# Two half borders in place of one: a chain of twelve layers on one core

## What is computed

```
for layer in range(2):                      # first_block
    h = rms_norm(x, norm_g[layer, 0]) * (1 + scale) + shift
    x = x + 0.5 * gate * swiglu(h, ffn_w_in[layer, 0], ffn_w_down[layer, 0])
    h = rms_norm(x, norm_g[layer, 1]) * (1 + scale) + shift
    y = diff_attention(h, ...) if layer == 0 else hgrn2(h, ...)
    x = x + gate * y
    h = rms_norm(x, norm_g[layer, 2]) * (1 + scale) + shift
    x = x + 0.5 * gate * swiglu(h, ffn_w_in[layer, 1], ffn_w_down[layer, 1])
h = rmsnorm(x, norm_g_2)                    # second_block
x = x + concat(gla, sparse attention, pool) @ w_out
return rmsnorm(x, final_norm_g)

rms_norm(h, g) = h * rsqrt(mean(h * h, axis=-1) + 1e-6) * g
swiglu(h, w_in, w_down): a, b = split(h @ w_in); (silu(a) * b) @ w_down     # d_ff = 2816
```

## Time and profile before

| | us |
|---|---|
| median of 3 runs | 2433.12 (2431.3 to 2435.06) |
| span of the profiled execution | 2435.2 |
| PE busy | 2385.0 (98%) |
| weight loads | 1908.2 (78%) |
| DVE busy | 1273.8 (52%) |
| ACT busy | 861.1 (35%) |
| POOL busy | 203.1 (8%) |

### The profile page before, as it was taken

How to read it: one execution, slowest core, us unless ns; L and a number is a source line. 1 busy time by engine, 2 the same in 40 slices (tenths; PEclk the granted TensorE clock), 3 DMA queues, 4 the chain that set the end, 5 groups by cost and what they waited for, 6 DMA issues and landing times.

```text
span 2435.2 us, 30379 instructions
## 1 busy us (share of the span) xinstructions
PE 2385.0 (98%) x11030; PEld 1908.2 (78%) x11030; DVE 1273.8 (52%) x1951; ACT 861.1 (35%) x1320; POOL 203.1 (8%) x337
## 2 busy tenths in 40 slices
PE   7999999999899999999999999999999999999998
PEld 4888888677588888888888878888888888867666
DVE  5886334455568883343333345554533333459554
ACT  3222223566443222232232243434432222344353
POOL 1212000000001110000000013331000000021100
PEclk9999999999999999999999999999999999999999
DMA  7899432321149983323333321222233333242221
GB/s 267 272 288 290 118 95 66 102 61 52 48 126 290 294 251 109 94 76 93 102 95 107 92 78 54 60 56 75 78 104 95 100 112 95 65 96 55 64 58 52
DMA packets 420386, 285.27 MB, mean 117 GB/s; under 512 B 22691, under 2 KB 397789, under 8 KB 420305
## 3 DMA queue, kind: packets, MB, share of 16 engines
q1 hardware_dynamic: 397888, 207.64, 29.4%
q0 software_dynamic: 20896, 73.80, 9.2%
q10 hardware_dynamic: 1520, 2.77, 0.3%
HBM read 281.85 MB, written 6.72 MB: 118 GB/s over the span
## 4 chain that ended last, share of the span: by engine, by line
PE 91%; DVE 3%; ACT 2%; DMA 1%; issue 1%; SPq 1%; POOL 0%; ACTq 0%; DVEq 0%; POOLq 0%
PE bank L666 13%; PE bank L667 13%; PE bank L668 13%; PE bank L834 7%; PE bank L836 7%; PE bank L835 7%; PE bank L1442 4%; PE bank L1444 4%; PE bank L1443 4%; PE bank L1469 2%; PE bank L701 2%; PE bank L703 2%; PE bank L702 1%; PE bank L1087 1%; PE bank L1114 1%; PE bank L681 1%
## 5 line engine op out<-in xcount | busy, mean ns | idle before, releaser
L624 DVE TENSOR_TENSOR w_lo<-raw,w_hi 128x1024 fp32r<-128x1024 f32 (+1 forms) x333 | 435.7, 1309 | 430.3 <-ACT w_hi L606 425.7
L606 ACT ACTIVATE w_hi<-raw 128x1024 fp32r<-128x1024 f32 (+1 forms) x333 | 371.8, 1117 | 479.9 <-PE bank L668 243.0
L666 PE MATMUL bank<-h_hi,w_hi 128*128 128x512 f32 x1344 | 523.1, 389 | 1.8 <-DVE w_lo L624 1.8
L667 PE MATMUL bank<-h_lo,w_hi 128*128 128x512 f32 x1344 | 522.9, 389 | 0.0
L668 PE MATMUL bank<-h_hi,w_lo 128*128 128x512 f32 x1344 | 522.8, 389 | 0.0
L666 PEld LDWEIGHTS bank<-h_hi,w_hi 128*128 128x128 f32 x1344 | 252.3, 188 | 55.3 <-DVE w_lo L624 2.7
L668 PEld LDWEIGHTS bank<-h_hi,w_lo 128*128 128x128 f32 x1344 | 252.3, 188 | 52.4
L667 PEld LDWEIGHTS bank<-h_lo,w_hi 128*128 128x128 f32 x1344 | 252.3, 188 | 52.0
L834 PE MATMUL bank<-g_hi,w_hi 128*128 128x512 f32 x704 | 277.8, 395 | 0.0
L836 PE MATMUL bank<-g_hi,w_lo 128*128 128x512 f32 x704 | 276.0, 392 | 0.0
L835 PE MATMUL bank<-g_lo,w_hi 128*128 128x512 f32 x704 | 273.2, 388 | 0.0
(11 more groups left out here) (407 smaller groups left out, 3056.5 us busy)
## 6 DMA issues: line engine op xcount, KB each, us to landing
raw<-in_ffn_w_in SPq DMA_DIRECT2D x176, 512.0 KB, 3.9
ada<-in_ada_w POOLq DMA_DIRECT2D x128, 512.0 KB, 5.0
raw<-in_ffn_w_down SPq DMA_DIRECT2D x64, 704.0 KB, 4.6
raw<-in_hgrn_w_in SPq DMA_DIRECT2D x32, 512.0 KB, 4.1
raw<-in_attn_w_qkv SPq DMA_DIRECT2D x24, 512.0 KB, 3.8
raw<-in_w_in SPq DMA_DIRECT2D x22, 512.0 KB, 3.8
ada_first<-in_ada_w SPq DMA_DIRECT2D x16, 512.0 KB, 10.8
bias_scratch<-bias_lines POOLq DMA_DIRECT2D x14, 320.0 KB, 9.1
```

The source lines that it names most:

```text
L606: line(nc.scalar.activation(w_hi[:, n % 2, 0:k * P], raw[:, n % 4, 0:k * P], ACT.Copy), hi_ready)
L624: line(nc.vector.tensor_tensor(w_lo[:, n % 2, 0:k * P], raw[:, n % 4, 0:k * P], w_hi[:, n % 2, 0:k * P].bitcast(F32), ALU.subtract), lo_ready)
L666: nc.tensor.matmul(out_ap, wh, xh, start=(k == 0), stop=False)
L667: nc.tensor.matmul(out_ap, wh, xl, start=False, stop=False)
```

## The change

Each border is now worked in two parts of 256 tokens. The last output block of an FFN (the last two of WO and HO) is multiplied first for tokens 0 to 255, into one bank, then for tokens 256 to 511, into another. Between the tiles of the second part TensorE runs the ones matmuls of the first (`sums_pe(pe, m, 0)`). ACT and DVE do residual, square, root, scaled tiles and high and low parts for the first part while TensorE multiplies the second. The next stage's first two blocks are multiplied for the first part (block N over 8 tiles, then N+1), with the ones matmuls of the second part before tile 4, and then for the second part, both blocks tile by tile as before (`pair_both`). The orders of ACT and DVE at a border are written out in `border_act` and `border_dve`, with the splits of N and N+1 among them. `idle_turns` is gone. The square of block j = 0 goes straight to `sumsq`, so its memset and one add go. The rolled loops of ACT and DVE over the down blocks are written out, and TensorE's covers j = 0 to 5. `POOLED` is empty, so the GpSimd code added does not run. Semaphore counts change to suit; those lines are left out below.

```diff
+        BORDER = {1: "F0", 2: "WO", 3: "F1", 4: "F2", 5: "HO", 6: "F3"}
+        STAGES = ("F0", "WO", "F1", "F2", "HO", "F3", "OUT")
+        TAKEN = {"WO": 10, "HO": 10}
+        ADDED = {"WO": 7, "HO": 7}
...
+        def half_bank(j, half):
+            if j == KD - 1:
+                return B[6] if half else B[3]
+            return B[4] if half else B[2]
+        def root_bank(half):
+            return B[7] if half else B[5]
...
+            if j == 0:
+                return
...
+            line(nc.scalar.activation(sq[:, :] if j else sumsq[:, :], xT[:, j, :], ACT.Square), sq_ready)
...
+        def residual_half_dve(dve, line, j, half):
+            c_ = cols_of(half)
+            line(nc.vector.scalar_tensor_tensor(out=xT[:, j, c_], in0=half_bank(j, half)[:, c_], scalar=gate_col[:, j:j + 1],
+                                                in1=xT[:, j, c_], op0=ALU.mult, op1=ALU.add), x_ready)
+        def add_half_dve(dve, line, half):
+            c_ = cols_of(half)
+            dve.wait_ge(sq_ready, line.value(x_ready))
+            line(nc.vector.tensor_tensor(sumsq[:, c_], sumsq[:, c_], sq[:, c_], ALU.add), sum_ready)
+        def square_half_act(act, line, count, j, half):
+            c_ = cols_of(half)
+            act.wait_ge(x_ready, count)
+            line(nc.scalar.activation(sq[:, c_], xT[:, j, c_], ACT.Square), sq_ready)
...
+        def pair_tile(pe, m, half, k, b, banks):
+            c_ = cols_of(half) if m else slice(0, T)
+            n = FIRST[NEXT[m]] + b
+            wh, wl = w_hi[:, n % 2, k * P:(k + 1) * P], w_lo[:, n % 2, k * P:(k + 1) * P]
+            pe.wait_ge(hhi_ready, tile_count(m, half, k))
+            nc.tensor.matmul(banks[b][:, c_], wh, h_hi[:, k, c_], start=(k == 0), stop=False)
+            nc.tensor.matmul(banks[b][:, c_], wl, h_hi[:, k, c_], start=False, stop=False)
+            pe.wait_ge(hpool_ready if pooled(m, k) else h_ready, low_count(m, half, k))
+            return nc.tensor.matmul(banks[b][:, c_], wh, h_lo[:, k, c_], start=False, stop=(k == KD - 1))
+        def pair_both(pe, m, half, banks):
+            for k in range(KD):
                 for b in range(2):
-                    s = (n + b) % 2
-                    nc.tensor.matmul(banks[b][:, :], w_hi[:, s, k * P:(k + 1) * P], xh, start=(k == 0), stop=False)
-                    nc.tensor.matmul(banks[b][:, :], w_lo[:, s, k * P:(k + 1) * P], xh, start=False, stop=False)
-                pe.wait_ge(h_ready, KD * m + k + 1)
-                for b in range(2):
-                    s = (n + b) % 2
-                    last = nc.tensor.matmul(banks[b][:, :], w_hi[:, s, k * P:(k + 1) * P], xl, start=False,
-                                            stop=(k == KD - 1))
+                    last = pair_tile(pe, m, half, k, b, banks)
...
+            xb = x_base(BORDER[m]) + TAKEN.get(BORDER[m], 9)
+            pe.wait_ge(lo_ready, n + 1)
+            pe.wait_ge(x_ready, xb - 1)
+            for k in range(KD):
+                if k == 4:
+                    sums_pe(pe, m, 1)
+                pair_tile(pe, m, 0, k, 0, banks)
+            pe.wait_ge(lo_ready, n + 2)
+            pe.wait_ge(x_ready, xb)
+            for k in range(KD):
+                pair_tile(pe, m, 0, k, 1, banks)
+            pair_both(pe, m, 1, banks)
...
-        def idle_turns(count):
-            for _ in range(count):
-                nc.tensor.matmul(B[7][:, 0:P], ones[:, :], ones[:, :], start=True, stop=True)
-        def norm_pe(pe, m):
-            pe.wait_ge(sum_ready, (KD - 1) * m)
-            nc.tensor.matmul(B[5][:, :], ones[:, :], sumsq[:, :], start=True, stop=False)
-            idle_turns(4)
...
+        def sums_pe(pe, m, half):
+            name, c_ = BORDER[m], cols_of(half)
+            sums = sum_base(name) + ADDED.get(name, 6)
+            squares = x_base(name) + TAKEN.get(name, 9)
+            pe.wait_ge(sum_ready, sums - 1 if halved(m) and half == 0 else sums)
+            nc.tensor.matmul(root_bank(half)[:, c_], ones[:, :], sumsq[:, c_], start=True, stop=False)
+            pe.wait_ge(sq_ready, squares if half else x_base(name) + KD)
+            nc.tensor.matmul(root_bank(half)[:, c_], ones[:, :], sq[:, c_], start=False, stop=True).then_inc(rms_ps, 1)
...
+        def border_act(act, line, m, after):
+            name = BORDER[m]
+            n, xb = FIRST[NEXT[m]], x_base(name)
+            split_hi(act, line, n - 1)
+            nc.scalar.preload_act_table_set("natural_log_exp_and_others")
+            if halved(m):
+                square_half_act(act, line, xb + 7, KD - 2, 0)
+                square_half_act(act, line, xb + 8, KD - 1, 0)
+                norm_root_act(act, line, m, 0)
+                norm_hi_act(act, line, m, 0, 0)
+                split_hi(act, line, n)
+                square_half_act(act, line, xb + 9, KD - 2, 1)
+                norm_hi_act(act, line, m, 0, 1)
+                norm_hi_act(act, line, m, 0, 2)
+                split_hi(act, line, n + 1)
+                square_half_act(act, line, xb + 10, KD - 1, 1)
+                norm_hi_act(act, line, m, 0, 3)
+            else:
+                square_half_act(act, line, xb + 8, KD - 1, 0)
+                norm_root_act(act, line, m, 0)
+                norm_hi_act(act, line, m, 0, 0)
+                norm_hi_act(act, line, m, 0, 1)
+                split_hi(act, line, n)
+                norm_hi_act(act, line, m, 0, 2)
+                norm_hi_act(act, line, m, 0, 3)
+                square_half_act(act, line, xb + 9, KD - 1, 1)
+                split_hi(act, line, n + 1)
+            norm_hi_act(act, line, m, 0, 4)
+            norm_root_act(act, line, m, 1)
+            for j in range(5, KD):
+                norm_hi_act(act, line, m, 0, j)
+            norm_rest_act(act, line, m, 1, after)
+        def border_dve(dve, line, m):
+            name = BORDER[m]
+            n = FIRST[NEXT[m]]
+            outs = sum(2 if halved(q) else 1 for q in range(1, m))
+            split_lo(dve, line, n - 1)
+            norm_scale_dve(dve, line, m)
+            if halved(m):
+                dve.wait_ge(half_out, outs + 1)
+                residual_half_dve(dve, line, KD - 2, 0)
+                add_half_dve(dve, line, 0)
+                dve.wait_ge(half_out, outs + 2)
+                residual_half_dve(dve, line, KD - 1, 0)
+                dve.wait_ge(rstd_ready, root_count(m, 0))
+                norm_tile_dve(dve, line, m, 0, 0)
+                dve.wait_ge(used, n - 1)
+                residual_half_dve(dve, line, KD - 2, 1)
+                norm_tile_dve(dve, line, m, 0, 1)
+                norm_low_dve(dve, line, m, 0, 0)
+                split_lo(dve, line, n)
+                norm_tile_dve(dve, line, m, 0, 2)
+                norm_low_dve(dve, line, m, 0, 1)
+                add_half_dve(dve, line, 1)
+                dve.wait_ge(used, n)
+                residual_half_dve(dve, line, KD - 1, 1)
+                norm_tile_dve(dve, line, m, 0, 3)
+                norm_low_dve(dve, line, m, 0, 2)
+            else:
+                dve.wait_ge(half_out, outs + 1)
+                residual_half_dve(dve, line, KD - 1, 0)
+                dve.wait_ge(rstd_ready, root_count(m, 0))
+                norm_tile_dve(dve, line, m, 0, 0)
+                norm_tile_dve(dve, line, m, 0, 1)
+                norm_low_dve(dve, line, m, 0, 0)
+                split_lo(dve, line, n)
+                norm_tile_dve(dve, line, m, 0, 2)
+                norm_low_dve(dve, line, m, 0, 1)
+                norm_tile_dve(dve, line, m, 0, 3)
+                norm_low_dve(dve, line, m, 0, 2)
+                dve.wait_ge(used, n)
+                residual_half_dve(dve, line, KD - 1, 1)
+            norm_tile_dve(dve, line, m, 0, 4)
+            norm_low_dve(dve, line, m, 0, 3)
+            norm_tile_dve(dve, line, m, 0, 5)
+            norm_low_dve(dve, line, m, 0, 4)
+            split_lo(dve, line, n + 1)
+            norm_tile_dve(dve, line, m, 0, 6)
+            norm_low_dve(dve, line, m, 0, 5)
+            norm_tile_dve(dve, line, m, 0, 7)
+            norm_low_dve(dve, line, m, 0, 6)
+            norm_low_dve(dve, line, m, 0, 7)
+            norm_rest_dve(dve, line, m, 1)
+            norm_gate_dve(dve, line, m)
...
-            with pe.Fori(0, KD // 2) as i:
+            with pe.Fori(0, KD // 2 - 1) as i:
                 for s in range(2):
-                    pe.wait_ge(x_ready, plus(i, 2, xb + s - 1))
-                    bank = B[s][:, :]
-                    for b in range(2):
-                        n = n0 + UP + 2 * s + b
-                        pe.wait_ge(lo_ready, plus(i, 4, n + 1))
-                        for k in range(KH):
-                            f = b * KH + k
-                            if f == KF - 1 and s == 0:
-                                pe.wait_ge(g_ready, 2 + KF * (fidx + 1))
-                            wh, wl = w_hi[:, n % 2, k * P:(k + 1) * P], w_lo[:, n % 2, k * P:(k + 1) * P]
```

(104 more changed lines are left out.)

226 lines of the change are left out of this document (132 added, 94 removed).

## The result

The changed kernel takes 2441.53 us (median of 8 runs, 2440.01 to 2444.71) against 2434.25 (8 runs) before; the ratio is 1.0031, 95% interval 1.0021 to 1.0041. Forecast were 2440.9 and +7.8 us; measured are +7.3.

A forecast was written before the change was run, and what follows sets the result against it. TensorE, busy 98%, bounds the kernel; only six border gaps, 36.9 us in all, could be won. Four FFN borders at 0.8 us plus WO and HO at 2.3 make 7.8 slower: 2433.1 + 7.8 = 2440.9 us, 8-in-10 range 2426 to 2451.

The forecast's parts named there:

- The new waits: Last block before a border: TensorE waits for block N-1's low part, 0.6 us at FFN, 0.95 at WO and HO.
- First 24 matmuls: Next stage's first-part matmuls, waiting on ACT and DVE: 3.8 us of work with 2.9 us of waits at FFN borders.
- Half matmuls: At the borders, 1296 matmuls of 256 columns, each with its own weight load, at 0.122 us each.
- the excess of 0.0155: 512-column matmul: 0.2288 us against 0.2133 for its cycles; excess taken as a cost per matmul, so a half takes 0.122.
- FFN borders were forecast at 33.0: Split stretch's start to pair's end at the four FFN borders: 33.0 us against 32.2 before, 0.8 slower each.
- WO at 30.4: Split stretch's start to pair's end at WO and HO: 30.4 us against 28.1 before, 2.3 slower each.
- a half matmul under 0.115: Sign of being wrong; the half-price rival (chance 0.18) put 256-column matmuls at 0.1144 us, total 2435.6.
- The clock: Rival, chance 0.08: TensorE's clock falls in the borders' new waits, 1.5 us lost a border, total 2450.
- The faster rival: Chance 0.23: ACT and DVE waits at borders don't form; 2429 us with waits halved, 2416 with none.

The follow-up runs named there:

- Experiments 3 to 6: Changed kernel: ACT, DVE and ones-matmul order rewritten, six borders 2426.05 us, FFN borders only 2426.27; weight block N-1 split earlier, in changed kernel 2436.53, in six-border reordered 2419.54.
- 5 and 6: Weight block N-1 split before the new x tile's square (ACT) and add (DVE): changed kernel 2436.53 us; same with ACT, DVE and ones-matmul order rewritten 2419.54 us.
- experiment 9: Kernel before the change without its 18 pad matmuls a border: 2450.57 us, ratio 1.0056 to the kernel before.
- experiment 8: Changed kernel with DVE forming only 8 of 1024 columns of block N+1's low part at each border: 2442.97 us, ratio 1.0033 to the kernel before.
- experiment 7: Kernel before the change with each of 2112 FFN down-stage matmuls made two of 256 columns, residual added in halves: 2439.19 us, ratio 1.0018.

## Why the prediction was right

*The new waits.* Forecast 0.6 and 0.95 on `w_lo`; the trace notes 0.55 and 0.89. First 24 matmuls: forecast 6.7 at an FFN border, 6.75 at F1 and F3 and 6.97 at F2 measured; at WO 8.1 forecast, 7.9 measured. Experiments 3 to 6 show that these waits are the loss, 5 and 6 that the early one lies on the path. This part of the mechanism was right.

*Half matmuls.* The term was too large: 0.122 forecast, 0.113 or 0.118 measured in the product stretches and 0.120 in the pair. It does not scale exactly with columns, nor is the excess of 0.0155 constant. With it FFN borders were forecast at 33.0 and came at 32.6, WO at 30.4 and came at 30.0: 2.4 us too much over six. The prediction named a half matmul under 0.115 as a sign of being wrong; in parts of the split stretches of F0, WO and F2 it was 0.113, in the rest 0.118.

*The clock.* I gave its fall 0.08 and expected none, since the waits are pieces. It fell at one border of six in the profile, and that 1.5 us made good most of the error above. At the rate of 7 in 24 an execution with six such borders loses 6 x 0.29 x 1.45 = 2.5 us, as much as the half matmuls were priced too high. Without it the borders add up to 5.5 us (4 x 0.4 + 1.9 + 2.0) and not 7.8. That the total came within 0.6 us is luck: two errors cancel. The Trainium skill ("TensorE: Matmul & The Clock Gate", HAM oscillation) says that gaps in TensorE's work bring the half clock; experiment 9 agrees for an empty gap, with 2.3 us a border. In the changed kernel the clock fell behind waits of at most 0.75 us each, and no run here isolates what decides it.

*What I passed over.* The faster rival needed no shorter operations: the order (of ACT, DVE and the ones matmuls together) was enough. I held the written order for fixed when I weighed it at 0.23, and for the kernel as it stands that was right.

## What to carry to other kernels

Splitting a serial stretch in two halves wins only what the helper engines can deliver in time, so walk their queues in the written order, operation by operation, before counting the gap as won. Put work that nobody waits for yet (a weight split, the second half's residual and root) behind the last operation that the busy engine does wait for, and work that it wants soon (experiments 5 and 6) ahead. A wait on one engine can be queueing on a third: taking work off the engine in between (experiment 8) won 0.3 us a border and nothing measurable in all. Where a forecast comes out right, check its terms one by one: here two wrong ones hid each other.

## What the runs showed of the hardware

A stream of fp32r matmuls of 256 columns runs at 0.113 us or at 0.118 in the same loop body, with the clock granted in full. Neither is half of 0.2288. In experiment 7 the speed holds for a whole stage (F0 and F1 against F2 and F3). In the split stretches it changes only where the stream is interrupted: in the changed kernel's trace, WO goes from 0.118 to 0.113 at the wait on `w_lo`, F0 and F2 at the ones matmuls, while F1, HO and F3 stay at 0.118 across both. What chooses between them stays open.
